# Cache attention of a hybrid decoder step: five finishing steps of the softmax moved one page later

## The reference, cut to what matters

```python
def scores(c, kr):
    k = mla_keys(c, kr, w_kb, k_norm_g)          # keys from latents, then an RMS norm per head
    return einsum('bqhe,blhe->bhql', q, k) * scale
def update(carry, sc, c):
    m_new = maximum(m, max(sc)); corr = exp(m - m_new); pr = exp(sc - m_new)
    return m_new, l * corr + sum(pr), acc * corr + einsum('bhql,blr->bhqr', pr, c)
# carry runs over the 16 pages and then the 4 new tokens
o_lat = acc / l
return einsum('bhqr,rhv->bqhv', o_lat, w_vb)
```

## Time and profile before

| | us |
|---|---|
| runs shown, median of 3 | 3636.77 (3636.39 to 3642.57) |
| the profiled execution, its own time | 3643.21 |
| its span, first to last instruction | 3641.4 |
| PE busy | 3072.2 (84%) |
| DVE, ACT, POOL busy | 1933.0, 1353.8, 1124.6 |
| cache attention, layer 1 | about 541 to 1089 of the span |
| cache attention, layer 2 | about 2346 to 2894 |

### The profile page before, as it was taken

One profiled execution on the slowest core, in us unless ns is written; L12 is line 12 of the kernel. 1 busy time (PEld: TensorE's weight loads), 2 busy tenths in 40 slices (PEclk: granted clock), 3 DMA queues, 4 the chain that ended last, 5 costly groups with the idle time before them and its releaser, 6 DMA issues. The chain is left out here.

```text
span 3641.4 us, 67385 instructions
## 1 busy us (share of the span) xinstructions
PE 3072.2 (84%) x26442; PEld 2723.6 (75%) x26442; DVE 1933.0 (53%) x3127; ACT 1353.8 (37%) x2146; POOL 1124.6 (31%) x720
## 2 busy tenths in 40 slices
PE   7668879999988879888885788699999788798888
PEld 7568548888877459787884784498888684697878
DVE  5463454555546455489155544454545465454991
ACT  3412344444433233333344133344444331333333
POOL 0031000999910000055501300029998000001554
PEclk8889889999988779999987899799999886798999
DMA  5101203111114146443350021122112230564433
GB/s 162 36 3 31 78 13 87 39 50 30 52 37 126 47 133 173 110 131 107 109 162 13 3 69 40 29 71 55 34 41 64 72 106 8 156 162 109 131 105 113
DMA packets 444032, 282.35 MB, mean 78 GB/s; under 512 B 64686, under 2 KB 439256, under 8 KB 443082
## 3 DMA queue, kind: packets, MB, share of 16 engines
q1 hardware_dynamic: 441492, 276.85, 26.9%
q10 hardware_dynamic: 2232, 1.26, 0.2%
HBM read 258.75 MB, written 19.29 MB: 76 GB/s over the span
## 5 line engine op out<-in xcount | busy, mean ns | idle before, releaser
L290 POOL TENSOR_TENSOR w_rests<-w_ring,w_heads 128x2048 fp32r<-128x2048 f32 (+1 forms) x76 | 306.9, 4042 | 1291.6 <-ACT w_heads L284 1291.6
L1245 PE MATMUL key_banks<-w_kb_head,latent_T_head 128*128 128x352 f32 x1536 | 518.8, 338 | 0.0
L1245 PE MATMUL key_banks<-w_kb_rest,latent_T_head 128*128 128x352 f32 x1536 | 496.6, 323 | 0.0
L1245 PE MATMUL key_banks<-w_kb_head,latent_T_rest 128*128 128x352 f32 x1536 | 496.2, 323 | 0.0
L1065 POOL TENSOR_TENSOR rwkv_state_tmp<-rwkv_state,vec 128x1024 f32<-128x1024 f32 x64 | 153.7, 2402 | 681.4 <-DMA rwkv_state<-in_state_rwkv_dram 676.5
L284 ACT CAST w_heads<-w_ring 128x2048 fp32r<-128x2048 f32 (+1 forms) x180 | 325.4, 1811 | 66.7 <-DMA w_ring<-in_w_in_dram 24.1
L1388 DVE TENSOR_REDUCE w_kb<-key_sq 128x8 f32<-128x1024 f32 x256 | 309.5, 1209 | 0.0
L1374 DVE TENSOR_TENSOR latent_T_rest<-turn_bank,latent_T_head 128x256 fp32r<-128x256 f32 x256 | 108.7, 425 | 367.0 <-ACT w_kb L1306 366.9
L1305 ACT CAST latent_T_head<-turn_bank 128x256 fp32r<-128x256 f32 x256 | 95.5, 373 | 558.5 <-PE turn_bank L1225 558.5
L1245 PEld LDWEIGHTS key_banks<-w_kb_rest,latent_T_head 128*128 128x128 f32 x1536 | 291.1, 190 | 0.0
L1245 PEld LDWEIGHTS key_banks<-w_kb_head,latent_T_head 128*128 128x128 f32 x1536 | 290.5, 189 | 0.1
(11 more groups left out here) (559 smaller groups left out, 7689.9 us busy)
## 6 DMA issues: line engine op xcount, KB each, us to landing
w_ring<-in_w_in_dram SPq DMA_DIRECT2D x48, 1024.0 KB, 5.5
w_ring<-in_ffn_w_up_dram SPq DMA_DIRECT2D x88, 512.0 KB, 5.0
latents<-in_cache_kv_latent_dram SPq DMA_DIRECT2D x256, 128.0 KB, 2.0
w_ring<-in_w_gate_dram SPq DMA_DIRECT2D x48, 512.0 KB, 4.0
w_ring<-in_ffn_w_down_dram SPq DMA_DIRECT2D x32, 384.0 KB, 3.7
w_ring<-in_ffn_w_down_dram SPq DMA_DIRECT2D x32, 320.0 KB, 4.1
rope_keys<-in_cache_k_rope_dram SPq DMA_DIRECT2D x256, 32.0 KB, 1.8
ssm_native<-in_state_ssm_dram SPq DMA_DIRECT2D x16, 512.0 KB, 7.1
```

Source lines behind the costliest of these rows:

```text
L290: ops.tensor_tensor(rests[:, slot, 0:tiles * P], ring[:, slot, 0:tiles * P], heads[:, slot, 0:tiles * P].bitcast(F32), ALU.subtract).then_ ...
L1245: last = nc.tensor.matmul(kbank[:, 3 * x + n, 0:KB], c[:, x, r * P:(r + 1) * P], w[:, r, cols], start=r == 0 and m == 0, stop=r == 1 and m ...
```

## The change

Only the numbers of the steps differ. TURN_TOP, SPREAD and SOFT, the four pages of VALUES, KEEP and FOLD each stand one page later; TOP stays at page 4 and DIVIDE at page 15. No instruction is added or removed.

```diff
     ROPE_AT = (10, 13)
     Q_AT = 8
     NEW = 0
-    TOTAL, LN, EXP, SCALE, TOP, TURN_TOP, SPREAD, SOFT = 0, 1, 2, 3, 4, 5, 6, 7
-    VALUES = {9: (0, 4), 10: (4, 8), 11: (8, 12), 12: (12, J)}
+    TOTAL, LN, EXP, SCALE, TOP, TURN_TOP, SPREAD, SOFT = 0, 1, 2, 3, 4, 6, 7, 8
+    VALUES = {10: (0, 4), 11: (4, 8), 12: (8, 12), 13: (12, J)}
     GROUPS = len(VALUES)
-    KEEP, FOLD, DIVIDE = 13, 14, 15
+    KEEP, FOLD, DIVIDE = 14, 15, 15
```

## The result

| | runs | median, us | ratio to before, 95% interval |
|---|---|---|---|
| before | 8 | 3636.88 (3635.58 to 3645.05) | 1 |
| changed | 8 | 3655.89 (3644.86 to 3662.37) | 1.0043 (1.0028 to 1.0059) |

The change makes the kernel about 0.4% slower, and the interval leaves out 1. The forecast was 3631.6 us, with a range to 3641.

What follows compares the result with a forecast made beforehand. PE, busy 374.4 of 382 us within the cache attention, was taken to set the pace. The terms -11.8 + 8.0 - 1.4 + 0 = -5.2 us, from 3636.8, gave 3631.6 us, with a range from 3625 to 3641.

Steps and rivals of the forecast that it cites:

- Term A: PE's fourteen waits for the maximum within the pages vanish with TURN_TOP one page later: -11.8 us.
- SPREAD, SOFT, VALUES, SP's queue: Moved steps keep their distances or find idle time, and later page loads keep a margin of about 9 us: cost 0.
- Term B: FOLD waits for KEEP, now behind the rotary sum, +0.67 us in 12 of 14 turns: +8.0 us, bounds +7 and +9.
- Term C: In the last sequence's tail, page 15's score comes 0.69 us earlier and FOLD falls into the gap: -1.4 us.
- Term D: Idle time at the four back edges, with a wait and FOLD now before the branch: 0 us, ends -4.6 and +12.9.
- The third rival: Wait before the branch holds the sequencer, which was a page ahead: +12.9, 3644.5 us; chance 0.11 for 2 us each or more.

Runs made afterwards that it cites:

- experiment 9: Kernel before with only TURN_TOP, SPREAD and SOFT one page later; VALUES, KEEP and FOLD not moved: 3632.43 us, ratio 0.9961.
- experiment 1: Changed kernel with KEEP back at page 13 and FOLD back at page 14: 3627.66 us, ratio 0.9958.
- experiment 2: Kernel before with FOLD alone moved to page 15, KEEP left at page 13: 3644.08 us, ratio 1.0001.
- experiment 3: Kernel before with only KEEP moved to page 14 and FOLD to page 15: 3664.23 us, ratio 1.0058.
- experiment 4: Changed kernel with the second half of the rotary squares at page 12 instead of 13, out of KEEP's way: 3640.93 us, ratio 0.9995.
- experiment 5: Changed kernel with its loop over the sequences written out, so no branch: 3632.71 us, ratio 0.9968.
- experiment 7: Kernel before with one added wait of PE for its own score at the end of page 15: 3665.51 us, ratio 1.0054.
- experiment 8: Kernel before with one added wait of PE for its own score at the end of page 13: 3645.84 us, ratio 1.0002.
- experiment 6: Kernel before with its loop over the sequences written out, so no branch: 3642.88 us, ratio 0.9996.
- experiment 11: Kernel before with an added wait of PE for its own score at page 15 and the loop written out: 3640.9 us, ratio 0.9986.

## Why the prediction was wrong

- **Term A, -11.8: right in its mechanism, 1 to 2 us too small.** The wait of L1257 for L1411 is left in the tails alone, and turned up nowhere else. Each tail's wait is 6.3 us instead of 7.2, since FOLD now lies in it. But the 0.05 us for each wait went the wrong way: in experiment 9 a plain sequence is 0.9 us shorter where the row of the wait says 0.80. The whole term comes to -13.7 in experiment 9 and -13.0 in experiment 1, idle times at the back edges set apart.
- **SPREAD, SOFT, VALUES, SP's queue, 0: right.** L1260 waits 7.2 us in all, L1268 no longer than before within the pages, and experiment 1 runs with the later loads at no cost.
- **Term B, +8.0: right.** L1274 waits 0.81 or 0.82 us in all twelve turns, forecast 0.79 to 0.87. Its total is 11.8 us and not some 13, because in the tails it waits 1.0 us instead of 1.4. In the last sequence FOLD waits for nothing:

```profile
1066.71 0.29 PEld L1249 LDWEIGHTS key_banks<-qr,w_kb 64*128 64x128 f32 x2 [0.22 <-issue]
1070.11 0.29 PEld L1249 LDWEIGHTS key_banks<-qr,w_kb 64*128 64x128 f32 x2 [0.22 <-issue]
1070.54 0.52 PEld L1274 LDWEIGHTS misc_bank<-fold_groups,latent_sums 128*128 128x128 f32 x4
```

- **Term C, -1.4: right.** The two scores above are 3.40 us apart, those of pages 14 and 15 before were 4.22 (from 1060.76 to 1064.98). The same 0.8 us is missing in both layers of every kernel with FOLD at page 15 (the changed one, experiments 2 to 5) and in no other, and what follows up to VALUES is as long as before: -1.6 us.
- **Term D, 0: this step failed.** The sentence was "The idle time is near the price of one block, so little seems to be hidden now." Measured: +9.1 us of idle time. It took the 0.96 us that a block's packet itself lasts for the price of the whole fetch; from the packet to the first instruction behind the branch it is 2.7 to 3.5 us (see below), most of which was hidden. The third rival, *The back edge loses its cover*, had the mechanism, and its bound of +12.9 holds the idle time; it got a chance of 0.11. Its own price for being slower, 1.3 us for each back edge, was passed with 2.3.
- **A term that was missing.** Even with D right, the sum would have been -5.2 + 9.1 = +3.9 us. Some 10 us more (9.8 by the rows) come from the granted clock, which falls to 1.2 GHz after each gap, and no term or rival asked what PE's clock does after a gap of 3 us or more in a stage that until then ran at 1.00 throughout.

The mechanism: PE's instruction stream runs ahead of the work that PE is doing, so the branch and the fetch behind it begin while page 15's matmuls are still at work, and 1 to 1.4 us are left to see. A wait that has to be sat out directly ahead of the branch stops the stream there. The DMA queue of instruction blocks, q8 in the earlier trace rows, shows when the fetch starts. In the kernel before and in the changed one, a packet of it is recorded between 740.8 and 740.9 us (first line before, second changed; packets, MB, and the packet's time as a share of 16 engines over this 0.1 us, so 0.96 and 1.4 us on one engine):

```profile
q8 instruction: 1, 0.02, 59.9%
q8 instruction: 1, 0.02, 88.2%
```

Before, this is 1.4 us ahead of page 15's score (742.24), while PE makes keys. In the changed kernel it is 2.1 us behind the score (738.66) and 1.0 us behind the end of the wait (739.77). The first load behind the branch follows 2.8 us after the packet before and 3.2 us after it in the changed kernel. Such a packet stands at all 36 back edges of the nine kernels that have them, 2.7 to 3.5 us ahead of that load. Where the wait was sat out (the changed kernel, experiments 3, 4 and 7) it comes 1.5 to 2.5 us after the score has started; in the kernel before and in experiments 1, 8 and 9 it comes 1.3 to 1.6 us ahead of the score, in experiment 2 0.8 to 1.0 ahead of FOLD. So the time from packet to load is much the same, and what the wait changes is when the fetch starts. The row doesn't name the engine that fetches; that it is PE rests on this distance, and on experiments 5, 6 and 11, which have no packet on q8 from 736 to 746 us.

From the end of the wait to the next load it is 744.03 - 739.77 = 4.3 us in the changed kernel, 4.5 in experiment 4 and 4.1 in 3 at the first back edge. In 7 it is 4.2, if the wait ends 0.47 us after the start of the score's load, as in experiment 11 (742.35 to 742.82). All sixteen such back edges lie between 3.9 and 4.5 us. If the packet follows the branch by 1.0 us in the kernel before too, the stream there is at the branch 2.4 us ahead of the score's load, and 2.7 us of the fetch are hidden; that is an estimate, since the trace doesn't show the branch itself.

The prediction named the rule of the Trainium skill on fetches ("Runtime: NRT & Kernel Launch", "Instruction fetch mechanics"), and that a taken branch makes the engine wait for its target agrees with experiments 5 and 11, where the branch and all gaps are gone. The Trainium skill, "TensorE: Matmul & The Clock Gate", in the table at its head, gives TensorE's queue 64 instructions. At a page's 36 loads and matmuls of keys in some 3.8 us that would be a lead of over 5 us, an estimate, and a fetch of 4.3 us would not be seen at all. The 1 us that stays in the kernel before and in experiment 8, and the packet that comes only 1.4 to 1.6 us ahead of the score there, don't bear out a lead of that length.

Still open: what sets how far the stream runs ahead, why the profiled executions differ by several microseconds outside the stage, and why the measured loss (0.28% to 0.59%, 10 to 21 us) tends to be larger than the stage's 9.2.

## What to carry to other kernels

Before placing a wait near the end of a loop body, look at the idle time behind the loop's branch: it is only what the engine's lead leaves of a longer fetch. Here a wait that really was sat out there, even one of 0.23 us, exposed all of it, while the same kind of wait two pages earlier cost 0.2 us a turn and nothing at the branch. Ask of every gap of some microseconds on a busy TensorE what the clock does after it, and give it a term of its own. And where a change moves several steps, price each alone: here three numbers bring the gain and two others the loss.

## What the runs showed of the hardware

- A hardware loop's back edge with this long body holds TensorE for 3.9 to 4.5 us from the end of a wait that was sat out ahead of it, and shows as 0.9 to 1.5 us of idle time where none was. The packet of instructions that belongs to it is recorded 2.7 to 3.5 us ahead of the first load behind the branch in either case.
- A semaphore wait that is already fulfilled leaves the stream its lead (experiment 2, 1.07 to 1.44 us); one of 0.23 us takes it away in full (experiment 4, 3.5 to 3.8 us).
- After idle gaps of 3.2 to 4.4 us at the back edges, the granted clock was down at 1.2 GHz for 3.4 to 6.8 us, part of it still in the gap, and key matmuls then started 0.30 us apart instead of 0.16. This was so at all four such gaps in the changed kernel and in experiments 3, 4 and 7, at one of the four short gaps in experiment 2, and at none in the kernel before and in experiments 1, 8 and 9.
